# RWKV scan of a two-block network: quarter layout of the array, transition products copied by ScalarE, identity as a second product

## The reference

```
def step(S, inp):
    r_t, w_t, k_t, v_t, a_t, b_t = inp
    sa = jnp.einsum('bhvk,bhk->bhv', S, a_t)
    S = S * w_t[:, :, None, :] + sa[..., None] * b_t[:, :, None, :] + v_t[..., None] * k_t[:, :, None, :]
    return S, jnp.einsum('bhvk,bhk->bhv', S, r_t)
```

## Time and profile before

| | us |
|---|---|
| median of 3 runs (lowest to highest) | 3154.09 (3149.60 to 3159.63) |
| the profiled execution | 3149.06 |
| its span, first to last instruction | 3146.9 |
| TensorE busy | 2876.5 (91%) |
| VectorE busy | 1134.7 (36%) |
| ScalarE busy | 942.3 (30%) |
| GpSimd busy | 778.9 (25%) |

### The profile page before, as it was taken

The page is one execution under the profiler, slowest core; times in us unless marked ns, Lnnn a source line. Parts: engine busy times, 40 slices in busy tenths (PEclk is TensorE's granted clock), DMA queues, the critical chain, the costliest instruction groups (busy, mean ns, idle before and its releaser), DMA issues. The chain is left out here.

```text
span 3146.9 us, 54449 instructions
## 1 busy us (share of the span) xinstructions
PE 2876.5 (91%) x24397; PEld 2238.6 (71%) x24397; DVE 1134.7 (36%) x1676; ACT 942.3 (30%) x1586; POOL 778.9 (25%) x218
## 2 busy tenths in 40 slices
PE   6987999999967898998899999997999989899998
PEld 4765888887855432333489989986788868678887
DVE  3434764654354300110455447363211123421111
ACT  3123233433323100000235554553322222132221
POOL 3320321220211000000132223222344424334442
PEclk8989999999988899999999999998999999999999
DMA  6111201011122599999521322222232223223321
GB/s 252 54 31 39 67 17 59 4 58 57 45 89 80 216 427 427 427 426 427 224 95 54 81 68 78 70 68 80 69 105 94 94 69 105 69 80 100 102 94 54
DMA packets 171627, 397.57 MB, mean 126 GB/s; under 512 B 9551, under 2 KB 99636, under 8 KB 146036
## 3 DMA queue, kind: packets, MB, share of 16 engines
q1 hardware_dynamic: 170416, 390.70, 33.9%
q10 hardware_dynamic: 980, 3.40, 0.3%
HBM read 387.71 MB, written 4.19 MB: 125 GB/s over the span
## 5 line engine op out<-in xcount | busy, mean ns | idle before, releaser
L179 POOL TENSOR_TENSOR weight_ring_lo<-weight_ring,weight_hi 128x2048 fp32r<-128x2048 f32 (+1 forms) x144 | 657.6, 4568 | 1995.6 <-ACT weight_hi L168 1956.3
L168 ACT CAST weight_hi<-weight_ring 128x2048 fp32r<-128x2048 f32 (+1 forms) x144 | 271.0, 1884 | 671.5 <-PE mlp_o L213 247.3
L213 PE MATMUL a_o<-weight_hi,latT_hi 128*128 128x512 f32 x576 | 176.7, 429 | 2.5 <-PEq L3325 2.5
L213 PE MATMUL a_o<-weight_ring_lo,latT_hi 128*128 128x512 f32 x576 | 158.2, 397 | 0.0
L213 PE MATMUL a_o<-weight_hi,latT_lo 128*128 128x512 f32 x576 | 157.7, 396 | 0.0
L1870 POOL TENSOR_TENSOR rws_E<-rws_AT,rw_tri 128x768 f32<-128x768 f32 x40 | 76.3, 1931 | 322.4 <-DVE rws_AT L1750 209.6
L213 PE MATMUL mlp_o<-weight_hi,mlp_hid_hi 128*128 128x512 f32 x512 | 138.8, 393 | 9.8 <-issue 9.8
L3201 DVE TENSOR_TENSOR x<-x,mlp_o 128x512 f32<-128x512 f32 x64 | 44.0, 687 | 281.4 <-PE mlp_o L213 281.4
L213 PEld LDWEIGHTS a_o<-weight_hi,latT_hi 128*128 128x128 f32 x576 | 133.0, 273 | 16.8 <-issue 8.2
L213 PEld LDWEIGHTS a_o<-weight_ring_lo,latT_hi 128*128 128x128 f32 x576 | 134.2, 270 | 8.1
L213 PEld LDWEIGHTS a_o<-weight_hi,latT_lo 128*128 128x128 f32 x576 | 134.2, 270 | 7.8
(11 more groups left out here) (617 smaller groups left out, 5801.7 us busy)
## 6 DMA issues: line engine op xcount, KB each, us to landing
weight_ring<-in_mlp_w SPq DMA_DIRECT2D x64, 1024.0 KB, 5.1
weight_ring<-in_a_wqkv SPq DMA_DIRECT2D x36, 1024.0 KB, 5.1
weight_ring<-in_w_up SPq DMA_DIRECT2D x32, 1024.0 KB, 20.3
weight_ring<-in_w_gate SPq DMA_DIRECT2D x31, 1024.0 KB, 22.1
weight_ring<-in_w_down SPq DMA_DIRECT2D x31, 1024.0 KB, 21.6
weight_ring<-in_w_mod SPq DMA_DIRECT2D x24, 1024.0 KB, 5.3
weight_hi_spare<-in_w_up SPq DMA_DIRECT2D x12, 1024.0 KB, 19.9
weight_hi_spare<-in_w_gate SPq DMA_DIRECT2D x12, 1024.0 KB, 22.3
```

Source lines behind the costliest of these rows:

```text
L168: self.nc.scalar.copy(self.view(self.hi[:, q % 2], p, True), self.view(self.slots[self.slot[p]], p, True)).then_inc(self.hi_ready, 1)
L179: self.nc.gpsimd.tensor_tensor(self.view(self.lo[:, s], p, True), self.view(self.slots[s], p, True), self.view(self.hi[:, q % 2], p, True) ...
L213: last = nc.tensor.matmul(dst, left(a, HK * r + k), right(b, k), start=(r + a + b + k == 0), stop=(r == 1 and a == 1 and k == HK - 1))
```

## The change

- **Layout.** A result may now lie on the other head's partitions. With s the chunk and h the head, `left` puts it on partitions of head h, in the slots of bank h xor (s mod 2); `right` puts it on the partitions h xor (s mod 2), in bank h. AT (the matrix), E, M, XA and XV lie left, MT, T, WV, At and ZV right. Products that read left and write right, or the reverse, go through `four_tiles`: rows and columns of four consecutive products are the four quarters. Products that read and write on the same side use `two_tiles` or `both_heads`. Each of them issues what it did.
- **SM**, a new job of TensorE, computes SB again into the right layout; VectorE makes MT from it straight out of PSUM. It stands behind SB; SK follows.
- **G** is copied by ScalarE, without the identity. RP no longer waits for it. Each S step has two products: the identity times S, and GT times S, added up in PSUM.
- **finish** is cut into seven steps, one behind each of S1 to S7 on VectorE. The gates come behind YV. The wait of TensorE for finish stands ahead of the turns of the mod rows.
- **ModPanels** writes four strips of 2 partitions (0, 32, 64, 96) with 64 moving columns each, into a bank of the states' regions, 4 units after each of S1 to S4 and S7 to S10. `keep` has four copies.

```diff
-    pe_jobs = ["SB", "SK", "SR", "KT", "M0", "BT", "AKV", "T1", "M1", "N1", "T2", "M2", "N2", "T3", "M3", "N3", "T4", "AT", "N4",
+    pe_jobs = ["SB", "SM", "SK", "SR", "KT", "M0", "BT", "AKV", "T1", "M1", "N1", "T2", "M2", "N2", "T3", "M3", "N3", "T4", "AT", "N4",
                "XA", "XV", "ZA", "ZV", "YA", "YV", "G", "H", "RP"] + states + ["Y"]
-    dve_jobs = ["SB", "SK", "SR", "MT", "M1", "N1", "M2", "N2", "M3", "N3", "N4", "YA", "YV", "G", "H", "RP"] + ["S0"] + states
-    act_jobs = ["KT", "M0", "BT", "AKV", "T1", "T2", "T3", "T4", "AT", "XA", "XV", "ZA", "ZV", "Y"]
+    dve_jobs = ["SB", "SM", "SK", "SR", "M1", "N1", "M2", "N2", "M3", "N3", "N4", "YA", "YV", "H", "RP"] + ["S0"] + states
+    act_jobs = ["KT", "M0", "BT", "AKV", "T1", "T2", "T3", "T4", "AT", "XA", "XV", "ZA", "ZV", "G", "Y"]
...
+        left = lambda h, s: (h, NB // 2 * (h ^ s & 1) + s // 2)
+        right = lambda h, s: (h ^ s & 1, NB // 2 * h + s // 2)
...
+        def four_tiles():
+            for s in range(0, NB, 2):
+                yield 0, s
+                yield 1, s
+                yield 0, s + 1
+                yield 1, s + 1
...
-                    last = product(name, d, E[lv % 2], M)
+                    last = product(name, d, E[lv % 2], left, M, left, right, four_tiles())
...
-                    last = product(name, d, MT, T1)
+                    last = product(name, d, MT, right, T1, right, left, four_tiles())
...
-                    last = product(name, d, T1, MT)
+                    last = product(name, d, T1, right, MT, right, right, two_tiles(0))
...
-                    last = mm(bank[region[name, d]][0][:, 0:HD], GT[d][:, s].rearrange("p h t -> p (h t)"), S[d][:, s], start=True, stop=True)
+                    dst = bank[region[name, d]][0][:, 0:HD]
+                    mm(dst, g.ident[:], S[d][:, s], start=True, stop=False)
+                    last = mm(dst, GT[d][:, s].rearrange("p h t -> p (h t)"), S[d][:, s], start=False, stop=True)
...
-                elif out and job == "YA":
+                elif out and job == "YV":
                     out.gates(pe)
-                elif job == "RP":
-                    if out:
-                        pe.wait_ge(out.step.sem, 7)
-                    elif prep:
-                        pe.wait_ge(prep.bonus_kept, 1)
-                    mods.rows_of(pe, 0, KD)
-                elif job[0] == "S":
-                    n, left = int(job[1:]), n_unit - KD
-                    mods.rows_of(pe, KD + left * (n - 1) // len(states), KD + left * n // len(states))
+                elif job in states[0:4]:
+                    n = states.index(job)
+                    mods.rows_of(pe, 4 * n, 4 * n + 4)
+                elif job in states[-4:]:
+                    n = states[-4:].index(job) + 4
+                    mods.rows_of(pe, 4 * n, 4 * n + 4)
...
-                elif name == "G":
-                    two = tri[:, 8, 0].unsqueeze(1).to_broadcast([P, NB // 2, CH])
-                    for b, c in enumerate(halves):
-                        for h in range(2):
-                            last = V.tensor_tensor(GT[d][head(h), c, h], part(d, name, b)[head(h)], two[head(h)], ALU.add)
...
-                elif out and job == "YV":
-                    out.finish(dve)
+                elif out and job in states[0:7]:
+                    out.finish(dve, states.index(job))
...
+                elif name == "G":
+                    for b, c in enumerate(halves):
+                        for h in range(2):
+                            last = nc.scalar.copy(GT[d][head(h), c, h], part(d, name, b)[head(h)])
```

More of the change, by code:

```diff
@@ L1433, in rows_of @@
                 self.w = self.g.stream.take(pe)
-            for i, h in enumerate(self.halves):
-                last = self.nc.tensor.matmul(self.part[h, n], self.g.silu[:, k, :], self.w[:, k, i * P:(i + 1) * P], start=(k == 0), stop=(k == KD - 1))
+            for i in range(4):
+                last = self.nc.tensor.matmul(self.part[32 * i:32 * i + 2, n], self.g.silu[:, k, :], self.w[:, k, i * HD:(i + 1) * HD],
+                                             start=(k == 0), stop=(k == KD - 1))
             if k == KD - 1:
@@ L1441, in keep @@
         act.wait_ge(self.g.stream.used, self.p0 + self.n_panel)
-        for h in self.halves:
-            last = self.nc.scalar.copy(self.rows[h], self.part[h])
+        for i in range(4):
+            last = self.nc.scalar.copy(self.rows[self.halves[i // 2], :, HD * (i % 2):HD * (i % 2 + 1)], self.part[32 * i:32 * i + 2])
         last.then_inc(self.kept, 1)
@@ L1530, in rwkv_scan @@
         eye = lambda h: g.ident[head(h), head(h)]
+        own = lambda h, s: (h, s)
+        left = lambda h, s: (h, NB // 2 * (h ^ s & 1) + s // 2)
+        right = lambda h, s: (h ^ s & 1, NB // 2 * h + s // 2)
+        at = lambda x, row, s: x[head(row), s]
         halves = [slice(0, NB // 2), slice(NB // 2, NB)]
@@ L1542, in both_heads, with two_tiles @@
                 yield 0, n + i
+        def four_tiles():
[4 more added lines that the diff above has]
+                yield 1, s + 1
+        def two_tiles(first):
+            for s in range(0, NB, 2):
+                yield 0, s
+                yield 1, s
+            for s in range(1, NB, 2):
+                yield first, s
+                yield 1 - first, s
         @block.tensor
@@ L1548, in _, with product @@
             act = lambda d, job: pe.wait_ge(act_done[d], act_jobs.index(job) + 1)
-            def product(name, d, left, right):
-                for h, s in both_heads(NB // 2):
-                    last = mm(cell(d, name, h, s, NB // 2), left[d][head(h), s], right[d][head(h), s], start=True, stop=True)
+            def product(name, d, x, xs, y, ys, outs, cells):
+                for h, s in cells:
+                    last = mm(cell(d, name, *outs(h, s), NB // 2), at(x[d], *xs(h, s)), at(y[d], *ys(h, s)), start=True, stop=True)
                 return last
@@ L1603, in run @@
                     pe.wait_ge(v_turned, 1)
-                    for h, s in both_heads(NB // 2):
-                        last = mm(cell(d, name, h, s, NB // 2), AK[d][head(h), s], Vt[head(h), s], start=True, stop=True)
+                    for h, s in four_tiles():
+                        last = mm(cell(d, name, *right(h, s), NB // 2), AK[d][head(h), s], Vt[head(h), s], start=True, stop=True)
                 elif name[0] == "T":
@@ L1677, in run @@
                 last.then_inc(pe_done[d], 1)
-            for d in range(2):
-                run("SB", d)
-                run("SK", d)
+            for job in pe_jobs[0:3]:
+                for d in range(2):
+                    run(job, d)
             if prep:
@@ L1690, in _ @@
             last.then_inc(v_placed, 1)
-            for job in pe_jobs[4:]:
+            for job in pe_jobs[5:]:
                 if prep and job == "BT":
@@ L1701, in _ @@
                     run(job, 0)
+                    if out:
+                        pe.wait_ge(out.step.sem, 7)
+                    elif prep:
+                        pe.wait_ge(prep.bonus_kept, 1)
                     mods.transpose(pe)
@@ L1786, in _ @@
                     run(job, d)
-                if prep and job == "MT":
+                if prep and job == "SR":
                     prep.squares(dve)
@@ L1915, in _ @@
             out.variance(dve)
-            out.finish(dve)
+            for i in range(7):
+                out.finish(dve, i)
 def project_rows(nc, g, name, part, x, norm_of, x_after=None, xn=None, junk=None, begun=None):
```

92 lines of the change are left out of this document (52 added, 40 removed).

## The result

The changed kernel takes 3125.1 us (median of 13 executions, 3115.5 to 3139.0) against 3153.2 (3147.2 to 3159.6, 13): ratio 0.992, interval 0.990 to 0.993. It is 28 us faster, where 78 were forecast. The profiled execution took 3122.4, its span 3120.6, 26 less than before. It is inside the range (3042 to 3126) at its very end, and that is luck: the upper end was made of half clocks and longer waits for ScalarE and VectorE, not of what held the kernel up. The mechanism that was to bring most of the gain brought little.

The account below looks back on a forecast made before the run. It took TensorE to bound the levels, with ScalarE and VectorE at 60 to 70% of its pace. Scans of -16.5, -20, -20 and -21.5 made -78 us, 3154.09 to 3076, range 3042 to 3126.

Parts of the forecast that it names:

- A four-quarter job takes 0.70 us: Product jobs of 24 products: four quarters start together every 0.058 us, so a job takes 0.70 us in place of 1.40.
- the quarters take turns: Rival, 9%: in four-quarter jobs four records cost 2 x 0.058, a job stays at 1.40 us; 3145 us in all.
- a load waits for its rows: Rival, 6%: in four-quarter jobs a weight load waits for its own rows' products, 2.6 us a job; 3308 us in all.
- The sum: Second scan by stages: front -3.3, levels to ZV -12.2, YA to first state -7.5, states +3.0; -20.0 us together.
- The 2.8 us of idling behind VectorE: Level 3, before N3's second job: TensorE idles 2.8 us for a bank while VectorE prepares the next head pair.
- YA to S1: Second scan's stretch from YA to the first state: 26.8 us now, 19.3 forecast, -7.5; H1 waits 2.1 for ScalarE.
- States, +3.0: Second scan's state stage: 12.8 us becomes 15.8, eight steps of 1.6 and two of 1.5, finish hidden in steps with units.
- The clock rival: Rival, 15%: idle gaps bring half clock, seven stretches of 7 us, up to 24 us lost; 3100 us in all.

Follow-up runs that it names:

- two at a time: The changed kernel with its four-quarter jobs issued two quarters at a time, same instructions in another order: 3135.4 us, ratio 0.994.
- shared loads: The changed kernel with XA and XV, ZA and ZV, YA and YV each made as one product: 3112.3 us, ratio 0.987.
- whole transposes: The shared loads kernel with KT, BT and V made by six whole-array products each, and the placement changed for that: 3129.1 us, ratio 0.992.
- the three with GpSimd's zeros: GT's zeros written by GpSimd in place of ScalarE: on shared loads 3112.3 us, on whole transposes 3119.1, on the changed kernel 3119.2.
- the filled kernels: Unread wide products in the state stage: changed kernel 3130.7 us; shared loads with GpSimd's zeros 3115.4; whole transposes with GpSimd's zeros 3093.6, every second step 3084.2.
- tail alone: The kernel before, still on two quarters, with only finish spread, gates behind YV, G on ScalarE, identity product and strips: 3140.0 us, ratio 0.996.

## Why the prediction was wrong, step by step

- **A four-quarter job takes 0.70 us: right.** Records in fours, 0.058 apart, no loss from sharing rows or columns, and loads hidden. The rivals that the quarters take turns, or that a load waits for its rows, are out. Starts within a four stand some 7 ns apart, so both rules of the Trainium skill that were weighed (TensorE: Matmul & The Clock Gate, Part 1 on the issue rate and Part 3 on what overlaps) are contradicted by this trace; the first points the right way, but what stands in its place here is a floor on the rate of instructions over a block.
- **"The sum", front and levels: wrong, and this is the step that failed.** I took TensorE's time from the array alone. A product of this size is four instructions, a job 96, and 96 instructions arrive in 1.40 us, whatever the array does. In the second scan the front gave 0.6 (forecast 3.3) and levels to ZV 5.4 (12.2), of which 1.4 is YA's first job, wrongly counted to them in the time before; the six jobs of a level, T, M and N for both directions, are 576 instructions, 576 x 14.5 ns = 8.4 us, and a level (T1 to T3, halved) takes 8.1 to 9.0 in the four scans, not 6.3. T1 to N4 as a whole hardly moved: 132.8 us in the four scans for 134.7 before. SM's 192 instructions, reckoned as 1.4 us of array time, are 2.8 by arrival. The front also had 3.4 us at half clock, from 528.5 on (0.94 in its mean, 1.00 before). The table says where the other 4.0 came from: 1.4 are T1's two jobs, 0.4 lie between T1 and N4, 2.2 between N4 and ZV. The 2.8 us of idling behind VectorE that I had put ahead of N3's second job were not there either: at the line of these products TensorE waited 0.5 us for VectorE in the whole scan.
- **YA to S1: right in size** in the scans with a finish (26.8 to 19.1; 19.3 forecast), for partly other reasons. H's second job waited 0.23 us for ScalarE, not 2.1, because TensorE came later; YA and YV took longer for want of instructions. In the first scan, where finish had not stood in the way, 3 us were forecast, and there was none: YV to S1 is 12.7 us for 12.6.
- **States, +3.0: right**, +2.3. Step 1.6, finish hidden, strips 0.41 us for four units (0.12 each forecast).
- **The clock rival was half right.** I had priced the half clock behind idle gaps, 7 us of it in seven places. It came elsewhere, in the state stage: 9 to 10 us at a time, in the profiles of six kernels that share the changed stage (two at a time, shared loads, whole transposes and the three with GpSimd's zeros), and, to go by the mean clocks, in 5 of 13 executions of the changed kernel. The steps with two or three wide mod units each ran at 1.00 in all four scans of the profile before; the change made the mod products thin and left two steps without any. That this is what lets the clock fall is argued from the filled kernels, not shown by itself. I had looked at what a step takes and given the state stage no clock term. What I had half right is small: four stretches of 3.4 us at half clock stand in the second to fourth scan of the profile after, where before three of 6.9 us stood behind H's wait for VectorE.

By scans: forecast -16.5, -20, -20, -21.5; measured +0.5, -11.5, -11.9, and -6.6 up to the end of Y. They make -29.5, and the later start of the first scan (+3.5) brings it to the 26 of the span. By parts: tail and states 13 to 14 (tail alone), four quarters about 15 of the 84 that the array could give.

How much of the changed kernel's median is due to the half clock stays open: eight undisturbed executions have a median of 3122, so some 3 us. What of the stage ahead of it makes the clock fall in some executions and not in others was not settled, nor whether fewer instructions in the levels would free the rest: each level product has its own stationary operand, and a kernel that left some out for a test was not run.

## What to carry to other kernels

Count instructions beside array time: where TensorE's products are small and run on quarters, work out the rate of its instructions (here 256 per 3.5 to 3.9 us, products and loads both counted) before pricing a better use of the array, and look for idle time put down to "issue" at equal counts. Then the way on is fewer and larger instructions, a shared stationary operand or a transpose on the whole array, and with them more of the quarters' gain comes through (N4 to YV in the four scans: 85.3 us before, 65.6 after the change, 42.7 with shared operands). Where a change thins the work beside a chain of short steps, look at the granted clock of that stage in more than one profile: here it cost 9 to 10 us each time it fell.

## What was not expected of the hardware

- Instruction arrival: 3.47 us per 256 on a quiet chip, 3.6 to 4.1 in the kernel's own stages. A block's packet starts 1.0 to 1.8 us after the first product of the block ahead, and its own first product comes 2.3 to 2.4 us after that; 1.9 us are enough to use one up.
- Products on other quarters start ahead of the program's order: with 12 products on two quarters ahead of 12 on the others, a job took 1.05 us, not 1.40, and with six ahead of six 0.66 to 0.77, nearly as in fours.
- Zero to four of four state stages at half clock (22.5 to 24.3 us for 14, once 17.7 where it stood for a part), with the same instructions in the stage, depending on kernel and execution. With some 16 wide products a scan added it stayed away, but for 1.2 us, in the profiles of two kernels and came in one stage of a third; the 12 of them inside the stage cost 2.2 us there, 0.19 each.
